# Two z projections between the levels, and the levels' query products on the Vector engine

## The reference, cut

```
p = h @ w_in                      # qkv, z, beta, a, hq, hf, hi, hgate, gate_dn, gate_hg
o_dn = gated_delta_rule(q, k, v, beta, g), forwards + backwards
o_dn = rmsnorm(o_dn) * dn_norm * silu(z)
o_hg = hgrn2_scan(silu(hq), k, hi, logf), forwards + backwards
o_hg = rmsnorm(o_hg) * hg_norm * silu(hgate)
merged = sigmoid(gate_dn) * (o_dn @ w_branch_dn) + sigmoid(gate_hg) * (o_hg @ w_branch_hg)
out = merged @ w_out
```

## Time and profile before

| what | us |
|---|---|
| median of 3 runs | 2311.51 (2311.47 to 2316.66) |
| the profiled execution, own time | 2303.78 |
| its span | 2301.6 |
| levels of the first mixer, PE busy of 99.5 | 86.8 |
| the same, DVE busy | 90.9 |
| the same, ACT / POOL busy | 48.9 / 59.9 |

### The profile page before, as it was taken

The page is one execution under the profiler, slowest core; times in us unless marked ns, Lnnn a source line. Parts: engine busy times, 40 slices in busy tenths (PEclk is TensorE's granted clock), DMA queues, the critical chain, the costliest instruction groups (busy, mean ns, idle before and its releaser), DMA issues.

```text
span 2301.6 us, 39173 instructions
## 1 busy us (share of the span) xinstructions
PE 2184.7 (95%) x15722; PEld 2038.9 (89%) x15722; DVE 1566.2 (68%) x2330; ACT 1064.4 (46%) x1504; POOL 191.6 (8%) x157
## 2 busy tenths in 40 slices
PE   7999989999999999999998998999999998999997
PEld 7998859989999998798997988898998988898996
DVE  4557657656575575667556689867767689867676
ACT  4335465533353345554333475434434475434442
POOL 0000000131000000000001007300000007300000
PEclk9999999999999999999999999999999999999999
DMA  6554424475555554344553442214554442214553
GB/s 251 188 182 165 165 74 165 153 214 184 208 194 187 188 191 146 128 147 166 185 191 139 165 147 92 74 56 149 190 189 167 165 147 92 74 62 168 183 183 126
DMA packets 52665, 359.10 MB, mean 156 GB/s; under 512 B 6400, under 2 KB 6784, under 8 KB 11072
## 3 DMA queue, kind: packets, MB, share of 16 engines
q1 hardware_dynamic: 46928, 340.81, 41.3%
q0 software_dynamic: 4336, 13.37, 2.1%
q10 hardware_dynamic: 1280, 3.19, 0.4%
HBM read 356.29 MB, written 1.05 MB: 155 GB/s over the span
## 4 chain that ended last, share of the span: by engine, by line
PE 79%; DVE 11%; ACT 4%; DMA 4%; issue 2%; SPq 0%; DVEq 0%; POOLq 0%; ACTq 0%
PE tile L754 43%; PE acc L787 18%; PE tile L767 7%; PE tile L1078 3%; DMA ring<-weights 3%; DVE ring_lo L1813 2%; PE tile L1269 2%; ACT w_hi L1340 2%; PE tile L923 1%; PE tile L897 1%; PE tile L802 1%; DVE work L2332 1%; DVE work L2303 1%; DVE bn L2198 0%; DVE work L2301 0%
## 5 line engine op out<-in xcount | busy, mean ns | idle before, releaser
L1813 DVE TENSOR_TENSOR ring_lo<-ring,w_hi 128x1024 fp32r<-128x1024 f32 x648 | 788.6, 1247 | 594.1 <-ACT w_hi L1340 591.9
L1340 ACT ACTIVATE w_hi<-ring 128x1024 fp32r<-128x1024 f32 x648 | 657.7, 1053 | 913.8 <-DMA ring<-weights 706.2
L754 PE MATMUL tile<-xT_hi,w_hi 128*128 128x256 f32 x3008 | 859.3, 286 | 25.7 <-DVE xT_lo L1804 13.9
L754 PE MATMUL tile<-xT_lo,w_hi 128*128 128x256 f32 x3008 | 854.2, 284 | 0.0
L754 PE MATMUL tile<-xT_hi,ring_lo 128*128 128x256 f32 x3008 | 854.0, 284 | 0.0
L754 PEld LDWEIGHTS tile<-xT_hi,w_hi 128*128 128x128 f32 x3008 | 580.3, 193 | 33.7 <-DVE ring_lo L1813 17.0
L754 PEld LDWEIGHTS tile<-xT_lo,w_hi 128*128 128x128 f32 x3008 | 580.5, 193 | 2.1
L754 PEld LDWEIGHTS tile<-xT_hi,ring_lo 128*128 128x128 f32 x3008 | 580.2, 193 | 0.0
L787 PE MATMUL acc<-w_hi,hidden_hi 128*128 128x512 f32 x528 | 206.6, 391 | 2.0 <-DVE ring_lo L1813 2.0
L787 PE MATMUL acc<-w_hi,hidden_lo 128*128 128x512 f32 x528 | 206.1, 390 | 0.0
L787 PE MATMUL acc<-ring_lo,hidden_hi 128*128 128x512 f32 x528 | 205.5, 389 | 0.0
(11 more groups left out here) (273 smaller groups left out, 2718.1 us busy)
## 6 DMA issues: line engine op xcount, KB each, us to landing
ring<-weights SPq DMA_DIRECT2D x324, 1024.0 KB, 4.8
work<-ln_g_rows POOLq DMA_DIRECT2D x8, 512.0 KB, 6.0
work<-ln_b_rows POOLq DMA_DIRECT2D x8, 512.0 KB, 7.2
work<-rpb POOLq DMA_DIRECT2D x32, 96.0 KB, 13.7
x<-x_in SPq DMA_DIRECT2D x1, 1024.0 KB, 8.0
work<-mem_in ACTq DMA_DIRECT2D x1, 1024.0 KB, 6.6
out<-x POOLq DMA_DIRECT2D x1, 1024.0 KB, 4.4
work<-hmask_in ACTq DMA_DIRECT2D x1, 840.0 KB, 8.3
```

The costliest lines, as they stand in the source:

```text
L754: j = mm(ps[:, f * S:(f + 1) * S], w[a][:, k, :], x2[b][:, k, :], start=(k == 0 and i == 0), stop=(k == KT - 1 and i == 2))
L1340: A(high_of(u, h), half_of(ring, u, h), ACT.Copy).then_inc(sems["w_hi"], 1)
L1813: V.tensor_tensor(half_of(ring_lo, u, h), half_of(ring, u, h), high_of(u, h).bitcast(F32), ALU.subtract).then_inc(sems["w_lo"], 1)
```

## The change

- The two z units leave the projections. Unit z0 stands behind gate 2 (level 2), z1 behind gate 5 (level 5), in the weight stream and on PE, ACT and DVE. ACT takes their tiles as plain copies; their Silu is one instruction over both, ahead of the gates' sigmoid, and POOL's gains for z come last.
- `square_sums` and `decay_sums` stand ahead of the hz units, the squares on ACT ahead of the taking of hi.
- `args(1)` on DVE stands behind the last split of the projections, not ahead of it.
- `qmul` is made by DVE, ahead of the next `args`.
- `near_start` moves from level 2 (between the halves of gate 2) to level 3, behind its gather; the first near row moves from between the halves of gate 3 to behind them, and one row moves behind z1.

The diff, cut:

```diff
-             ("hi", 0), ("hi", 1), ("hz", 0), ("hz", 1), ("z", 0), ("z", 1))
+             ("hi", 0), ("hi", 1), ("hz", 0), ("hz", 1))
...
-NEAR_AFTER_HALF = ((3, 0), (3, 1), (4, 0), (4, 1), (5, 0), (5, 1), (6, 0), (6, 1), (7, 0))
+Z_AT = {2: 0, 5: 1}
+NEAR_AFTER_Z = (5,)
+NEAR_AFTER_HALF = ((3, 1), (4, 0), (4, 1), (5, 0), (5, 1), (6, 0), (6, 1), (7, 0))
...
@@ PE, mixer2
-                for name in ("hi", "hz"):
-                    for j in range(2):
-                        project(name, j)
+                for j in range(2):
+                    project("hi", j)
                 square_sums()
                 decay_sums()
                 for j in range(2):
-                    project("z", j)
+                    project("hz", j)
...
+                    if k in Z_AT:
+                        project("z", Z_AT[k])
+                    if k in NEAR_AFTER_Z:
+                        near_row(next(rows))
...
@@ ACT, mixer2
-                for j in range(2):
-                    feed_one("hi", j)
-                    if j == 0:
-                        silu_qkv(5)
-                    take(T[("hi", l, j)], tok2(hi, j))
+                feed_one("hi", 0)
+                silu_qkv(5)
                 act.wait_ge(sems["qkv_silu"], 6 * l + 4)
                 for j in range(4):
                     A(pair(l2s, j), pair(qkvT, j), ACT.Square).then_inc(sems["l2_sq"], 1)
-                for j in range(2):
-                    feed_one("hz", j)
-                    silu_tokens(T[("hz", l, j)], tok2(hz, j))
+                take(T[("hi", l, 0)], tok2(hi, 0))
+                feed_one("hi", 1)
+                take(T[("hi", l, 1)], tok2(hi, 1))
...
                 for j in range(2):
-                    feed_one("z", j)
-                    silu_tokens(T[("z", l, j)], tok2(zs, j))
+                    feed_one("hz", j)
+                    silu_tokens(T[("hz", l, j)], tok2(hz, j))
...
+                    if k in Z_AT:
+                        feed_one("z", Z_AT[k])
+                        t = T[("z", l, Z_AT[k])]
+                        take(t, tok2(zs, Z_AT[k]), lambda ps: ps.rearrange("p (t c) -> p t c", t=TT))
...
                     if v == LEVELS - 1:
+                        for j in range(2):
+                            act.wait_ge(*taken(T[("z", l, j)]))
+                        A(zs, zs, ACT.Silu).then_inc(sems["z_silu"], 1)
...
@@ DVE
+            def qmul(l, k):
+
+                Q, m = hKQ[:, (k - 1) % 2, 1, :], min(1 << (k - 1), P)
+                dve.wait_ge(sems["hg_exp"], (LEVELS + 2) * l + k + 1)
+                if k == 1:
+                    dve.wait_ge(sems["hg_qs"], l + 1)
+                Q4 = Q.rearrange("p (n u m) -> p n u m", u=2, m=m)
+                V.tensor_tensor(Q4, Q4, pairs_of(qs_both, 0, m, 4 * S + m), ALU.mult).then_inc(sems["hg_q"], 1)
...
-                feed_one("z", 1)
+                feed_one("hz", 1)
+                args(l, 1)
...
+                        if half == 0 and k <= LEVELS:
+                            qmul(l, k + 1)
                         if half == 0 and k < LEVELS:
                             args(l, k + 2)
-                        if half == 1 and k == 2:
+                        if half == 0 and k == 3:
                             near_start()
...
+                    if k in Z_AT:
+                        feed_one("z", Z_AT[k])
+                    if k in NEAR_AFTER_Z:
+                        near_step(next(rows))
...
@@ POOL, mixer2
-                for k in range(1, 3):
-                    qmul(k)
-                    decays_of(2 * k - 2)
-                    decays_of(2 * k - 1)
-                qmul(3)
+                for g in range(4):
+                    decays_of(g)
...
-                qmul(4)
                 level_masks(NEAR)
-                qmul(5)
                 row_gains("hz", hz, 1)
-                qmul(6)
-                row_gains("z", zs, 0)
-                qmul(7)
-                qmul(8)
                 level_masks(NEAR + 1)
                 level_masks(NEAR + 2)
+                row_gains("z", zs, 0)
```

26 lines of the change are left out of this document (13 added, 13 removed).

## The result

The changed kernel takes 2321.68 us (median of 7 runs, 2320.11 to 2333.75) where the kernel before takes 2310.95 (7 runs, 2304.35 to 2316.66): ratio 1.0054, 95% interval 1.0039 to 1.0069. A second set of twelve runs, taken later beside other variants, gave 1.0025 (1.0009 to 1.0040), 2318.94 against 2311.46. By these two ratios the change costs some 6 to 12 us. The forecast was a gain of 3.3 us, 2308.2, with 2294 to 2319 as its range: wrong in sign, the first set outside the range and the second at its very end.

The account below looks back on a forecast made before the run. PE was taken as the bound ahead of the levels, DVE within them. Per mixer −10.9 + 7.0 for the levels + 2.3 for the Silu gave −1.6, for two −3.3: 2311.5 to 2308.2 us, range 2294 to 2319.

Parts of the forecast that it names:

- Projections, -10.9: Ahead of the levels: with the z units gone, level 0 starts 10.9 us earlier per mixer (low 9, high 11.6).
- args(1) and the lead: Between the projections' last split and gather 0: args(1) adds 2.85 us on DVE, cutting the lead from 10.9 to 8.0.
- Query products, +9.4 and -10: DVE in the levels: eight products add 9.4 us, stalls behind POOL worth 10.0 us go; nearly nothing left in sum.
- The walk through the levels: DVE gather to gather: 37.9, 24.9, 14.65, then 21.5 us to the first inverse's end; lead falls to 3.9.
- The place of DVE's wait: Behind gate 5, ahead of the splits behind z1: DVE should be idle for some 3 us.
- Silu of z, +2.3: Ahead of the gates' sigmoid: one table load (1.28) and one pass (1.05) lengthen the chain by 2.3 us, uncovered.
- the sum itself: Whole kernel: −3.9 + 2.3 = −1.6 us per mixer, −3.3 for two, giving 2308.2 against the median.
- the levels, entered as +7.0: Level 0 to the inverse: the levels grow by 10.9 − 3.9 = 7.0 us per mixer.
- the 108 that the forecast named as its failure: Levels from level 0 on: about 106.5 us expected, 99.5 before; over 108 means failure.
- A: Levels: PE's idle time takes all z units, so 8.6 us per mixer is gained, 2294.3; chance 0.24.
- B: Levels 2 and 5: z units hide nothing because of DVE's order, +5.9 us per mixer, 2323.2; chance 0.09.
- C: Levels: POOL's 22 remaining operations still stop DVE as much, up to +3.4 us per mixer, near 2318; chance 0.13.

Follow-up runs that it names:

- c1_after_again: The changed kernel, unedited, timed again beside its variants: 2318.94 us, ratio 1.0025 to the kernel before.
- e10_after_warm: Changed kernel plus unread PE products of 512 columns, two in the inverse and six ahead of the wait behind Silu and sigmoid: 2311.17 us, ratio 0.9996.
- e8_z1_projected: Changed kernel with only the second z unit back in the projections, its Silu still behind the levels: 2313.79 us, ratio 0.9999.
- e11_e9_warm: e9 plus two unread PE products of 512 columns in the inverse: 2295.43 us, ratio 0.9928.
- e2_products_dve: Kernel before with only the query products moved from POOL to DVE: 2312.60 us, ratio 1.0002.
- e4_products_pool: Changed kernel with only the query products back on POOL: 2324.03 us, ratio 1.0050.
- e13_before_warm: Kernel before plus two unread PE products of 512 columns in the inverse: 2309.95 us, ratio 0.9991.
- e9: e8_z1_projected with z1's Silu in the projections, z0's at the start of level 8, POOL's z gains behind DVE's state-key products: 2299.44 us, ratio 0.9950.
- e5: Changed kernel with z's Silu ahead of the inverse's last level and POOL's z gains held until the inverse's last tiles are taken: 2317.69 us, ratio 1.0018.
- e12: Changed kernel plus only two unread PE products of 512 columns in the inverse: 2312.26 us, ratio 1.0000.
- e14: Changed kernel plus only three unread PE products ahead of the wait behind Silu and sigmoid: 2316.81 us, ratio 1.0020.
- e1_silu_early: Changed kernel with only the Silu of z moved ahead of the last level of the inverse: 2318.26 us, ratio 1.0020.

## Why the forecast was wrong

The three parts of a mixer, in us, from the traces (in brackets the time at half speed, which the profile's clock has more finely than its column of two digits). The first runs from ACT's scaling of the queries to level 0, the others are those of the rows above:

| kernel | to level 0 | levels | behind the levels |
|---|---|---|---|
| before | 36.9, 37.0 | 95.2 (6.8), 95.4 (6.8) | 52.3 (6.8), 49.0 (0) |
| forecast | -10.9 | +7.0 | +2.3 |
| after | 25.8, 25.8 | 104.8 (6.8), 103.6 (3.4) | 54.6 (6.8), 57.2 (13.7) |
| c1_after_again | 25.8, 27.3 (3.4) | 104.8 (6.8), 104.8 (6.8) | 58.8 (17.1), 58.7 (17.1) |
| e10_after_warm | 25.8, 25.8 | 104.6 (6.8), 102.6 (0) | 53.9 (0), 53.9 (0) |
| e8_z1_projected | 31.6, 33.0 (3.4) | 93.9 (0), 94.0 (0) | 57.1 (13.7), 54.7 (6.8) |
| e11_e9_warm | 31.5, 33.0 (3.4) | 93.9 (0), 93.9 (0) | 49.8 (0), 49.8 (0) |

*Projections, -10.9.* Right: -11.1 and -11.2. In c1_after_again the second mixer has a fall of 3.4 us there, and 1.5 less is won.

*args(1) and the lead.* Right: level 0 starts 11.1 and 11.2 earlier and the first gather 7.9 and 8.4 (it was 39.7 behind the scaling of the queries, and is 31.7 and 31.4). The wait for the exponential is there too.

*Query products, +9.4 and -10.* Right in sum. The rows are 1.2, but for the first (1.54) and two beside POOL (2.32, 2.18). e2_products_dve has a net of +1.2 busy us and levels 1 to 1.7 us shorter; e4_products_pool has them longer by 2 to 4. The Trainium skill's rule ("Perfetto Trace Analysis", section "Optimizing Scalar/DVE Operations"), that moving work between GpSimd and the Vector engine might not help, agrees as far as the time goes: 1.0002 for the products alone. The slower time that I had derived from it did not come.

*The walk through the levels.* Gather 0 to 3: 38.4 (forecast 37.9), 3 to 5: 24.1 (24.9), 5 to 6: 16.3 and 15.3 (14.65), 6 to the end of the first inverse: 22.5 (21.5). The place of DVE's wait, 3 us behind z1, was right, and 3.63 long. Where the clock did not fall, 5 to 6 took 14.9 (e10_after_warm, second mixer), which is the forecast. What the walk left out is that z0's splits wait too (2.42, forecast none). Both waits end on the transfer, not on PE, which the trace of before shows nowhere in the levels, since no two units follow each other there; it does show it right ahead of them, behind the two z units, where ACT waits 2.02 us for a landing at 1897.28. This costs 0.5 to 0.7 over PE's own release, as far as the rows tell; it was not tried alone.

*Silu of z, +2.3.* Its own size is right: 2.37 on ACT, and the stretch behind the levels is 2.3 longer at the same clock (52.3 and 54.6, one fall each). The trace again has 1.28 for a table load and the next activation 0.01 behind it, without the draining of 1.38 us that the Trainium skill ("ScalarE: Activation LUTs", section "What ACT_TABLE_LOAD costs") adds. With it the sum would have been nearer to the result, for a wrong reason.

*The step that failed* is the sum itself: it took every duration of PE at the clock of before, and nothing in it priced the clock. The Silu of z went in as +2.3 of length and nothing more. But it also made PE's wait 3.15 us instead of 0.79, and behind the longer wait the clock fell in 7 of 12 mixers, behind the shorter in none of 12. In the stretches such a fall of 6.8 us costs 2.4 to 2.6 (e8 57.1 against 54.7, after 57.2 against 54.6). With work of PE in both places the loss is gone: 0.9996 (0.9983 to 1.0008) against 1.0025 (1.0009 to 1.0040) for after in the same job. There the median clock of after is 0.9795 and of before 0.983, and 0.001 goes with 1.4 us over the runs of before: that is 4.9 us, most of what the second set lost.

The stretch behind the levels was entered as +2.3 and came out at +5.3 on average in the first trace (55.9 against 50.6). Of this 2.3 is the Silu, some 1.3 the fall behind the wait in one mixer of two, and the rest, 1.7, chance: before's second mixer had no fall in its inverse, which most mixers of every kernel have. The +8.1 of c1_after_again is that of its slowest run. What could have told stands in the trace of before: the stretch behind the levels is at clock 0.93 in one mixer and at 1.00 in the other, and even the levels are at 0.97 in the forecast's own. The clock of this code was not something to take as given.

*A second term was too small*: the levels, entered as +7.0, came out at +9.6 and +8.3. The clock has little part in it, for before's levels have 6.8 us at half speed too; up to 1.4 of the first mixer's is a fall in level 5. Against the forecast the pieces of the first mixer are +0.3 to the first gather, then +0.5, -0.8, +1.6 and +1.0. To the start of PE's long row of the inverse, where 99.5 was counted from, the levels last 109.1 and 107.9: one beyond the 108 that the forecast named as its failure, the other just below.

How near the rest came can be told by an estimate from the rows. e10_after_warm has 53.9 behind the levels, 2.6 more than 49.0 + 2.3; without the added products it would be at 2306. e13_before_warm has 49.8, 0.8 more than 49.0, and would be at 2308.4. So at full clock in that stretch the change would gain some 2.4 us, and the forecast was 3.3. The intervals of both are wider than this, so it isn't shown.

*The rivals.* A (all of z hidden) is true for z0 and false for z1. I named 2294.3 for it; e9, with z0 alone between the levels and nothing on the chain, has 2299.4. B named DVE's splits behind z as the mechanism and 8.6 us of growth as the turning point. The splits did wait at both places, 2.42 and 3.63 us, and the levels grew by 9.6 and 8.3. But at z0 it cost nothing (e8 and e9), and at z1 what bounds the stretch is PE, busy for 15.5 of 16.3 us, not DVE's order. C did not occur in the time, though single rows of 2.2 to 2.3 us beside POOL stayed.

*The profiled time of before.* Its 2303.8 us lie at the low end of its runs (median 2311). The largest reason is a stretch of unchanged code: between 250 and 350 us its clock is 0.98, and in after 0.86. Of the seventeen traces four have 0.98 there (before, e5, e12, e14) and thirteen 0.86, and it doesn't go with what was changed. Of before, then of after:

```profile
250.00:350.00 100.00, 83.50 (x564) 69.47 (x563) 62.37 (x148) 57.31 (x139) 0.00 (x0) 0.98 0.26 94
```

```profile
250.00:350.00 100.00, 86.93 (x535) 70.14 (x535) 61.09 (x147) 54.98 (x136) 0.00 (x0) 0.86 0.25 94
```

That is 7 us of offset at 356 us, 9.6 by the start of the first part in the table, all ahead of anything the change touches. Of the 17.8 us between the two traces only 6.1 lie in the parts of the table, and the sum rightly stood against the median. It also tells how large the clock's chance is: over the runs of before in one job, 0.001 less of mean clock goes with 1.3 to 1.4 us more. The median clock of after is 0.979 to 0.9795, of before 0.982 to 0.984.

What stays open: why the clock of the unchanged stretches differs from look to look, why a wait of 3.15 us brings a fall in some mixers and not in others, and how much of the gap between the two sets of after (1.0054 and 1.0025) is just that. The transfer's share of the two waits behind z was not taken away by itself.

## What to carry to other kernels

A unit of work hides only where its own engine waits, so place it by that engine's idle time in the very stretch, not by the mean over a stage. Here one of two equal units was hidden whole and the other not at all. Before a wait is lengthened or work taken from PE, read the granted clock of that stretch in more than one mixer or run. Where it falls in one of them, 2.4 us more of wait can bring as much again with it, and cheap unread products can hold the clock. An operation of POOL cost DVE's chain nearly its full length (2.1 and 2.2 us of 2.3) in the two places where DVE was waited for, so look at what will stand beside it. In e5_gain_late a semaphore only moved it to the second such place.

## What the runs showed of the hardware

Not expected was that added work makes a kernel faster. Two unread products of 0.94 us ahead of the products of 64 columns left no fall in the inverse in any of the eight mixers that have them (e10, e11, e12, e13), where 24 of 26 without them have it. With them after has 1.0000 where it had 1.0025, and the best version 0.9928 where it had 0.9950; each pair of intervals overlaps, so the times show less than the rows do. And the clock falls where PE counts as busy: in the inverse for 49 of 52 us. PE had waited 0.8 us for DVE before it, and was at matmuls of 64 columns, which take about as long (0.117 us each) as those of 128 (0.112). No run tells the wait and the short matmuls apart.

A fall shows in the rows as matmuls that take twice as long: in c1_after_again 32 of 64 columns took 6.91 us, not 3.76, and behind the wait of 3.16 us 64 matmuls took 10.76. In after's first mixer the same 64 took 3.96 and 3.98 behind the same wait.

DVE and POOL take turns in whole operations, as the earlier trace rows had it, and now with a single one moved about: four rows of DVE went from 3.60 us to 5.71 beside POOL's 2.33 (e1_silu_early), and two from 1.29 (e2_products_dve) to 3.45 (e5_gain_late).
